# Row numbers from short lists, query units behind later lots, and a convolution whose mean products stand between its taps

## The reference

```python
def conformer_conv(h, w_pw1, b_pw1, w_dw, b_dw, ln_g, ln_b, w_pw2, b_pw2):
    a, gate = jnp.split(h @ w_pw1 + b_pw1, 2, axis=-1)
    y = a * jax.nn.sigmoid(gate)
    y = lax.conv_general_dilated(y, w_dw[:, None, :], window_strides=(1,),   # 31 taps
                                 padding=[(CONV_K // 2, CONV_K // 2)],
                                 dimension_numbers=('NWC', 'WIO', 'NWC'),
                                 feature_group_count=CONV_W) + b_dw
    y = jax.nn.silu(layernorm(y, ln_g, ln_b))
    return y @ w_pw2 + b_pw2                    # then x = x + g1 * y
...
        q = (hc @ w_query).reshape(B, T_CHUNK, PEER_HEADS, 2, PEER_DKEY // 2)
        s = jnp.einsum('bthpd,hpnd->bthpn', q, sub_keys).astype(jnp.float32)
        s_top, i_top = lax.top_k(s, PEER_TOPK)                       # 16 of 128, twice a head
        cand = (s_top[..., 0, :, None] + s_top[..., 1, None, :]).reshape(B, T_CHUNK, PEER_HEADS, PEER_TOPK * PEER_TOPK)
        cand_idx = (i_top[..., 0, :, None] * PEER_NKEYS + i_top[..., 1, None, :]).reshape(cand.shape)
        g_s, pos = lax.top_k(cand, PEER_TOPK)                        # 16 of 256
        e_idx = jnp.take_along_axis(cand_idx, pos, axis=-1)
        g = jax.nn.softmax(g_s, axis=-1)
        u = u_emb[e_idx]
        act = jax.nn.gelu(jnp.einsum('btd,bthkd->bthk', hc, u).astype(jnp.float32), approximate=False)
        return jnp.einsum('bthk,bthkd->btd', (g * act).astype(h.dtype), v_emb[e_idx])
```

## Time and profile before

| | us |
|---|---|
| median of 3 runs | 1574.71 |
| lowest and highest | 1573.56, 1574.86 |
| profiled execution | 1576.96 |
| its span in the trace | 1575.6 |
| PE, DVE, ACT, POOL busy | 1396.1, 1210.9, 733.0, 342.8 |
| mean granted clock of PE | 0.983 |

### The profile page before, as it was taken

How to read it: one execution, slowest core, us unless ns; L and a number is a source line. 1 busy time by engine, 2 the same in 40 slices (tenths; PEclk the granted TensorE clock), 3 DMA queues, 4 the chain that set the end, 5 groups by cost and what they waited for, 6 DMA issues and landing times.

```text
span 1575.6 us, 20772 instructions
## 1 busy us (share of the span) xinstructions
PE 1396.1 (89%) x7570; PEld 1022.9 (65%) x7570; DVE 1210.9 (77%) x2374; ACT 733.0 (47%) x1644; POOL 342.8 (22%) x313
## 2 busy tenths in 40 slices
PE   9899999999999999999999979978777677777776
PEld 3778899999987899998888855633332232322232
DVE  6977788887997788887785797777777777777654
ACT  4555465455577655545354544443333333333323
POOL 1100000001000000003010144555454343444430
PEclk9999999999999999999999989999999999999999
DMA  9755359998520499993432399999999999999995
GB/s 390 309 214 174 121 209 351 354 350 314 186 81 21 145 351 363 336 335 112 156 111 104 121 363 420 420 419 420 420 420 420 421 420 420 420 421 420 421 420 239
DMA packets 66199, 477.15 MB, mean 303 GB/s; under 512 B 7345, under 2 KB 7345, under 8 KB 8881
## 3 DMA queue, kind: packets, MB, share of 16 engines
q0 software_dynamic: 36864, 268.45, 41.2%
q1 hardware_dynamic: 29232, 207.37, 35.6%
q10 hardware_dynamic: 2, 0.01, 0.0%
HBM read 474.75 MB, written 1.05 MB: 302 GB/s over the span
## 4 chain that ended last, share of the span: by engine, by line
PE 49%; DMA 26%; DVE 18%; ACT 3%; issue 2%; POOL 2%; SPq 0%; DVEq 0%; POOLq 0%; ACTq 0%
DMA ring<-in_uv,crow 13%; PE ps L2054 7%; DMA row_x<-in_uv,crow 6%; PE ps L1645 6%; PE ps L1646 6%; PE ps L1647 6%; DVE HID L805 4%; PE ps L1940 4%; PE ps L1939 4%; PE ps L1937 4%; DMA row_w<-in_uv,crow 4%; DVE WB L477 3%; DMA HID<-in_uv,crow 2%; PE ps L1631 2%; DVE ring L1041 2%
## 5 line engine op out<-in xcount | busy, mean ns | idle before, releaser
L477 DVE TENSOR_TENSOR WB<-ring,WB 128x1024 fp32r<-128x1024 f32 x232 | 287.6, 1240 | 48.8 <-ACT WB L1128 45.5
L1128 ACT ACTIVATE WB<-ring 128x1024 fp32r<-128x1024 f32 x232 | 243.6, 1052 | 123.9 <-PE ps L1940 85.0
L1645 PE MATMUL ps<-hH,WB 128*128 128x256 f32 x928 | 269.7, 291 | 5.6 <-DVE WB L477 2.8
L2054 PE MATMUL ps<-ring,P 128*128 128x512 f32 x448 | 211.3, 616 | 66.9 <-ACT P L1463 66.9
L1646 PE MATMUL ps<-hL,WB 128*128 128x256 f32 x928 | 262.9, 283 | 0.0
L1647 PE MATMUL ps<-hH,WB 128*128 128x256 f32 x928 | 262.8, 283 | 0.0
L2054 PEld LDWEIGHTS ps<-ring,P 128*128 128x128 f32 x448 | 83.6, 195 | 188.8 <-ACT P L1463 102.8
L1453 ACT ACTIVATE On<-On 128x2 f32<-128x2 f32 x127 | 25.8, 203 | 375.5 <-DVE On L1041 375.5
L1041 DVE CUSTOM_DVE_ANT_0 ring<-ring,cT 128x1024 f32<-128x1024 f32 x112 | 136.3, 1225 | 77.6 <-DMA ring<-in_uv,crow 74.6
L1645 PEld LDWEIGHTS ps<-hH,WB 128*128 128x128 f32 x928 | 178.1, 192 | 10.9 <-issue 6.3
L1646 PEld LDWEIGHTS ps<-hL,WB 128*128 128x128 f32 x928 | 178.1, 192 | 2.2 <-issue 2.1
(11 more groups left out here) (304 smaller groups left out, 2747.0 us busy)
## 6 DMA issues: line engine op xcount, KB each, us to landing
ring<-in_stream SPq DMA_DIRECT2D x116, 1024.0 KB, 6.5
ring<-in_um SPq DMA_DIRECT2D x66, 1024.0 KB, 7.5
ring<-in_wm SPq DMA_DIRECT2D x4, 1024.0 KB, 12.8
bias<-in_bias SPq DMA_DIRECT2D x2, 2048.0 KB, 15.4
HID<-in_um SPq DMA_DIRECT2D x4, 512.0 KB, 17.9
ring<-in_uv,crow POOLq DMA_INDIRECT x112, 27.9
xT<-in_xT SPq DMA_DIRECT2D x1, 1024.0 KB, 8.8
cT<-in_cxT SPq DMA_DIRECT2D x1, 1024.0 KB, 14.6
```

The costliest lines, as they stand in the source:

```text
L477: ve.tensor_tensor(unit_dst(j, 1), unit_src(j), f(unit_dst(j, 0)), ALU.subtract).then_inc(s_lo, 1)
L1128: se.activation(unit_dst(j, 0), unit_src(j), ACT.Copy).then_inc(s_hi, 1)
L1645: te.matmul(o, wh[:, c], hi[:, kt, :], start=(kt == 0), stop=False)
L2054: mm = te.matmul(ps[4 + 2 * n + q][:, :], diag[:, g % 8, :], row_ap[row_of[g]][:, 1024 + q * 512:1536 + q * 512], start=(g % 128 == 0), st ...
```

## The change

In the expert layer, the first eight row numbers of route 0 come from short lists: the largest of all pair sums has to lie among the eight best of both lists, as do the seven behind it, so `first_eight` takes the eight best of either list, their 64 sums and the eight best of these. Lots 0 to 3 wait for these alone (`dve_route_first_eight`). `second_eights` then completes both lists and route 0 goes on as before; only eight of its row numbers are written by it. Before the first dot VectorE now does route 0 and the splits up to `W0+7`. Route 1 follows in steps behind dots 0 to 4, and up to lot 14 a step stands behind every dot. Queries 6 to 15 stand behind lots 3, 4, 6, 8, ... 20 (`query_lot`), five unread products ahead of mix 0, and `G1` is 50.

The last two pairs of the stream no longer go through `ring` in this stage: units 12 and 13 are loaded into `late` (which joins what were `bsp`, `wsp` and `g2row`) when the first pair of `pw2` has been split, unit 14 into a part of `bias` behind the loads for the scores, unit 15, half a pair, when the pair `L0+4` has been split. The unread products read `cols` in place of `bsp`.

In the convolution, ScalarE goes on with the next channel's diagonals and empties a channel eight diagonals later; six of the eight mean products stand between taps 14 to 19 of the last channel; one unread product follows the mean. Gate times bias is added to `xT` by VectorE ahead of the product (L865 of the change), and the product with `w_pw2` goes from PSUM into `xT` in one instruction of VectorE (L883). ScalarE converts a unit ahead of the squares, and up to the sixth tile VectorE's split stands ahead of the residual.

```diff
-        NROW, G1 = 14, 44
+        NROW, G1 = 14, 50
+        query_lot = dict(zip(range(6, 16), (3, 4, 6, 8, 10, 12, 14, 16, 18, 20)))
+        query_at = {l: k for k, l in query_lot.items()}
...
             for kt in range(8):
                 ve.tensor_tensor(yc[:, kt, :], yc[:, kt, :], ps[7][:, 0:256], ALU.subtract).then_inc(s_cen, 1)
+            for kt in range(8):
+                V.then_inc(ve.tensor_scalar(xT[:, kt, :], xT[:, kt, :], ab[:, 4, kt:kt + 1], None, ALU.add))
+            gb_in = V.n
...
-                    kt = 4 * b + u
-                    V.wait_ge(*out_a["pw2", b, u, 0])
-                    x_done.then_inc(ve.tensor_tensor(xT[:, kt, :], xT[:, kt, :], ptmp[:, kt, :], ALU.add), ("pw2", kt))
-                    unit(first["pw2", b] + u)
+                    kt, name = 4 * b + u, ("pw2", b, u, 0)
+                    if kt < 6:
+                        unit(first["pw2", b] + u)
+                    V.wait_ge(*dense[name])
...
+                    out_v.then_inc(ve.scalar_tensor_tensor(out=xT[:, kt, :], in0=row_bank(name)[:, 0:256],
+                                                           scalar=M[:, 1, 16 + kt:17 + kt], in1=xT[:, kt, :],
+                                                           op0=ALU.mult, op1=ALU.add), name)
+                    if kt >= 6:
+                        unit(first["pw2", b] + u)
...
+            def second_eights():
+                for j in range(2):
+                    V.then_inc(ve.match_replace(wk, st[:, j, 0:8], sS[0][:, j, :], GONE))
+                    V.wait_own()
+                    V.then_inc(ve.max(st[:, j, 8:16], wk))
+                    V.wait_own()
+                    V.then_inc(ve.max_index(ix[:, j, 8:16], st[:, j, 8:16], wk))
+                    V.wait_own()
+                V.then_inc(ve.tensor_copy(ixf[:, 0:2, 8:16], ix[:, 0:2, 8:16]))
+                V.wait_own()
...
             route = route_steps()
             V.wait_ge(s_const, 5)
-            for i in range(10):
+            for i in range(5):
                 next(route)
-                if i % 2 == 0:
-                    split_to(4 + i // 2)
-            split_to(9)
+                split_to(4 + i)
             for l in range(128):
                 dot(l)
-                if l % 2 == 0 and 2 <= l <= 14:
-                    split_to(l // 2 + 9)
+                if l == 3:
+                    split_to(9)
+                if l - 3 in query_at and query_at[l - 3] <= 12:
+                    split_to(query_at[l - 3] + 4)
...
-                if l % 8 < 5:
+                if l < 15 or l > 15 and l % 8 < 5:
...
-            for c, kt in enumerate(CP):
-                for k in range(31):
-                    d = 31 * c + k
-                    if d >= 8:
-                        S.wait_ge(s_tap, d - 7)
+            for d in range(len(TAPS) + 8):
+                if d >= 8:
+                    S.wait_ge(s_tap, d - 7)
+                if d < len(TAPS):
+                    kt, k = TAPS[d]
                     se.activation(dg[:, d % 8, :], ident[:], ACT.Copy, scale=wdw[:, k, kt:kt + 1]).then_inc(s_diag, 1)
-                S.wait_ge(s_tap, 31 * c + 31)
-                y_a.then_inc(se.activation(yc[:, kt, :], ps[4 + c][:, 0:256], ACT.Identity, bias=col["bdw"][:, kt:kt + 1]), kt)
+                if d in conv_emptied:
+                    kt = conv_emptied[d]
+                    y_a.then_inc(se.activation(yc[:, kt, :], ps[4 + CP.index(kt)][:, 0:256], ACT.Identity,
+                                               bias=col["bdw"][:, kt:kt + 1]), kt)
             sqrt_next()
+            ahead(first["pw2", 0])
...
-            query(6)
-            ahead(W0 + 7)
-            chosen(1)
             for l in range(128):
                 (gelu if l < 127 else gelu_last)(l)
-                if l % 2 == 0 and 2 <= l <= 18:
-                    query(l // 2 + 6)
-                    ahead(W0 + l // 2 + 7)
-                if l % 4 == 0 and 4 <= l <= 20:
-                    key_scores(l // 4 + 2)
+                if l - 1 in query_at:
+                    k = query_at[l - 1]
+                    query(k)
+                    ahead(W0 + k + 1)
+                    if k % 2:
+                        key_scores(k // 2)
...
-                G.wait_ge(s_eu, 8 * n + h + 1)
+                if l < 4:
+                    G.wait_ge(s_eu8, 1)
+                else:
+                    G.wait_ge(s_eu, 8 * n + h + 1)
...
+            for d, (kt, k) in enumerate(TAPS):
+                if k == 0:
+                    T.wait_ge(*out_v["pw1", kt // 2, 2 * (kt % 2) + 1, 0])
+                T.wait_ge(s_diag, d + 1)
+                te.matmul(ps[4 + CP.index(kt)][:, 0:256], dg[:, d % 8, :], yp[:, kt, k:k + 256],
+                          start=(k == 0), stop=(k == 30)).then_inc(s_tap, 1)
+                if kt == CP[-1] and 14 <= k < 20:
+                    mean_product(means[k - 14])
+            for kt in means[6:]:
+                mm = mean_product(kt)
             mm.then_inc(s_mean, 1)
+            T.wait_ge(s_cols, 16)
+            stand_in(ps[3], cols[:, 0:512], 1)
...
-            query(6)
+            stand_in(ps[5], cols[:, 0:512], 5)
             for l in range(128):
                 mix(l)
-                if l % 2 and l <= 17:
-                    query(7 + l // 2)
-                if l % 4 == 3 and l <= 19:
-                    key_scores(l // 4 + 3)
+                if l in query_at:
+                    query(query_at[l])
+                    if query_at[l] % 2:
+                        key_scores(query_at[l] // 2)
...
-                    elif i in (L0 + 4, L0 + 5):
-                        pair(i + 2)
+                    elif i == L0 + 4:
+                        sp.dma_start(unit_src(W0 + 15), A["stream"][L0 + 7][:, 1024:2048]).then_inc(s_late[2], 16)
...
+                        sp.dma_start(unit_src(W0 + 14), A["stream"][L0 + 7][:, 0:1024]).then_inc(s_late[1], 16)
+                    if 2 * i == first["pw2", 0]:
+                        P.wait_ge(*g_out[1])
+                        sp.dma_start(late[:], A["stream"][L0 + 6]).then_inc(s_late[0], 16)
```

More of the change, by code:

```diff
@@ L283, in mod_in, with in_ring @@
             return s_slot[4 + q % 2], 16 * (q // 2 + 2)
+        def in_ring(i):
+            return i < W0 + 12
         def unit_src(i):
+            if not in_ring(i):
+                return (late[:, 0:1024], late[:, 1024:2048], bias[:, 3072:4096], ring[:, pair_slot(L0 + 4), 0:1024])[i - W0 - 12]
             return ring[:, pair_slot(i // 2), i % 2 * 1024:i % 2 * 1024 + 1024]
@@ L289, in unit_dst, with unit_in @@
             return WB[:, i % 3, half, :]
+        s_late = [sem(f"last_query_{n}_in") for n in ("pair", "unit_14", "unit_15")]
+        def unit_in(i):
+            if in_ring(i):
+                return pair_in(i // 2)
+            return s_late[max(0, i - W0 - 13)], 16
         s_const, s_cols, s_x, s_row_c, s_c = sem("const"), sem("cols_in"), sem("x_in"), sem("crow_in"), sem("ctx_in")
@@ L313, in program @@
         m0_out = Steps(sem("dve_mod0"), ["c", "cc", "ca"])
-        x_done = Steps(sem("dve_x"), [("mlp0", k) for k in range(8)] + [("pw2", k) for k in range(8)]
+        x_done = Steps(sem("dve_x"), [("mlp0", k) for k in range(8)]
                        + [("mlp1", k) for k in range(8)] + [("fin", k) for k in range(8)])
@@ L393, in x_ready @@
             if n == "mlp1":
-                return x_done["pw2", k]
+                return out_v["pw2", k // 4, k % 4, 0]
             if n in ("fin", "b2"):
@@ L990, in route_steps @@
                     V.wait_ge(s_sc2, 2 * h + n + 1)
-                    for k in range(2):
+                    if r == 0:
+                        first_eight()
+                        yield
+                        second_eights()
+                    for k in range(2) if r else ():
                         j = 2 * h + k
```

82 lines of the change are left out of this document (48 added, 34 removed).

## The result

| | before | change |
|---|---|---|
| median of 5 runs, us | 1574.71 | 1567.67 |
| lowest and highest | 1573.56, 1577.87 | 1564.88, 1569.28 |
| profiled execution, its span | 1576.96, 1575.6 | 1569.28, 1568.0 |
| PE, DVE, ACT, POOL busy | 1396.1, 1210.9, 733.0, 342.8 | 1400.9, 1215.2, 734.4, 338.7 |

What follows compares the result with a forecast made beforehand. DMA's gathered bytes at 420.5 GB/s were taken to bound the kernel from 940 us on, TensorE before; 8.5 + 1.25 - 1.0 + 2.2 = 10.95 us gave 1566.0 profiled, 1563.8 as median, range 1560 to 1568 (1570 with Rival A).

Steps and rivals of the forecast that it cites:

- Sooner start: Start of the gather stage: row numbers from short lists come at 896.6 instead of 905.2, 8.5 us sooner (7.1 to 9.0).
- Weights out of the stage: Gather stage: fewer weight bytes move among the gathers, 0.53 MB less, 1.25 us gained (0 to 3.75).
- Dry time: Eight-row stretch: DMA waits behind TensorE's mixes and queries, 3.5 us lost (1 to 7) against 2.5 now, 1.0 worse.
- A sign that the prediction had named for being wrong: Gather stage: DMA under 400 GB/s in several stretches of 5 us between 960 and 1030 us.
- Rival A: Lots 4 to 24: the eight-row loop starves DMA throughout, 9 us lost instead of 3.5, time 1569.5; chance 0.15.
- The convolution: Convolution through the second mlp's root: reordered products, additions, conversions and splits gain 2.2 us (0.5 to 3.5).
- it passes on whole: Behind the convolution: TensorE is busy without a hole, so the whole 2.2 us gain reaches later stages.
- Rival B: Eight-row stretch: TensorE's clock falls to 1.2 GHz, 5 us lost a lot with a query, three give 1579; chance 0.04.
- C: Lots 22 to 24, now on eight rows instead of fourteen, each lose 3 us, time 1573; chance 0.06.
- rule on the shared port: Gather stage: denser route steps on VectorE would hold back GpSimd's gathers, time 1.5 us over the forecast; not adopted.

Runs made afterwards that it cites:

- whole_route: The changed kernel without its short lists, so all first gathers wait for route 0's sixteen row numbers; 0.9968 of the kernel before.
- late_pair_in_stage: The changed kernel with the weights of units 12 and 13 loaded inside the gather stage, not at the convolution; 0.9927 of the kernel before.
- change_again: The changed kernel itself, unaltered, run again beside the follow-up kernels; 0.9925 of the kernel before.
- lookup_alone: The changed kernel with the convolution's edits, from the taps to the residual of w_pw2, taken back; 0.9946 of the kernel before.
- unread_in_holes: The changed kernel with two unread products in each of two TensorE holes in the last attention; 0.9908 of the kernel before.
- conv_alone: The kernel before with only the convolution's part of the change; 0.9981 of the kernel before.

## Why the prediction was right, and where its sizes were off

**Sooner start, 8.5.** Measured 8.63 (12.91 less 4.28). Dot 0 was expected at 912.0 and came at 910.58, mix 0 at 916.2 and came at 915.32. That this is worth its full length was the sum's silent assumption. whole_route shows 0.5 to 0.6 of it in this kernel; the rest is the pair of weights that now meets the gathers and the dry time, which the sum counts in terms of their own, below.

**Weights out of the stage, 1.25.** The bytes left as stated: from the first gather to the end 271.41 MB, before 271.93. But late_pair_in_stage shows the price of 2.4 us per MB to be wrong here: nearly 0, since dry time follows.

**Dry time, "I take 3.5 us lost in all".** This is the term that was mis-sized: 6.5 in the profile, 5.3 in change_again's (50.46 less 48.21 MB), inside the bounds 1 and 7. A sign that the prediction had named for being wrong came with it, under 400 GB/s in several stretches of 5 us: 6 of the 14 from 960 to 1030 us, the lowest 283. The working had two lots with a query and scores at 10.6 us, from the 7.30 us of the earlier trace rows (its terms add up to 10.7). Measured it is 11.4 (996.10 to 1007.49), without scores 9.7. In the kernel before the scores stood behind a query of the next head. Now they stand right behind their own second query, and TensorE waits for ScalarE to empty it, in the view of waits from 940 to 1040 us:

```profile
PE ps L2135 <- ACT HID L1233: 2.6, 5, 0.5
```

A query with scores takes 4.5 us (11.39 less two mixes, 6.87), where the earlier trace rows gave 3.87: 0.65 more for each of five heads, 3.3 us, about what the term was short. That this wait is the reason is argued from the sizes; no run moved the scores alone. The order of the instructions had shown it, had I asked of each wait in a new place whether what it waits for is still being made. Rival A thus happened in part, in size between its 9 and my 3.5. Spreading the queries takes the dry time from 6.5 (47.73 MB) to 1.4 us (49.87 MB) and the time down by 3.3 to 5.4 us.

**The stage in all.** From the route's start to the end the sum had -8.75 (8.5 + 1.25 - 1.0). The profile has -6.8, the other profiles with the same stage -7.6 (late pair), -8.1, -8.3, -8.3 and, without the unread products, -8.9. With the dry time of 6.5 one expects -5.9. The 1 us between this and the profile lies ahead of the first full slice, where the sum has no term. From the first gather's issue to 940 us DMA moved 17.44 MB in 43.96 us in the change and 12.01 MB in 34.51 us before; at 420.5 GB/s that is 2.5 us lost, where it was 6.0, and of these 6.0 the prediction had counted 2.5 and left out the 3.4 up to 908.9, for which the change has 2.5. In the other profiles up to 2 us more stay open: lookup_alone and unread_in_holes, by the same sum at -6.5 and -6.2, end at -8.3. They moved 23.00 and 23.12 MB in the last 70 us, the change 22.18, so the difference lies in how the last rows land; why it varies no run shows.

**The convolution, 2.2.** Root 2.22 sooner, of 2.5 from the first tap on (0.3 was lost ahead of it); centring 1.02 sooner, where 1.45 was expected, since the product of the last-emptied channel waits 0.65 for ScalarE; the additions took 2.19 of the 2.7 allowed. "Behind it TensorE is busy without a hole, so it passes on whole" is false as it stands: there are two holes of 1.7 us, behind which the clock falls or not. In the profile of the change that took 1.4 of the 2.2 back, in conv_alone's it gave 3.2 more; by the ratios the part is worth 3.0 (1.6 to 4.3), which fits the 2.5 to 4.0 at the root.

So the 3.3 us between forecast and profile are 2.0 in the stage and 1.4 of clock. That the two ratios lie on either side of the forecast's 0.9931 is in part luck: the dry time was 1.8 to 3 us too small, and against it stood 1 us at the first gather that the sum did not have, a convolution worth up to 4.0 at the root, and an end of the stage that varies by up to 2 us. Rival B did not happen: the clock is 1.00 from 905 to 1040 us. Nor did C: from 1050 us on DMA moves 419 GB/s. The Trainium skill's rule on the shared port (SBUF — State Buffer, "SBUF: two separate sides"), by which GpSimd can't write a gather's descriptors while VectorE holds the port with a copy-like fp32 operation, shows little here when VectorE's work gets denser: of the gathers from 905 to 1100 us 26 of 80 took over 1.3 us to issue, before 23 of 83.

## What to carry to other kernels

A stage that one resource bounds at last may be bound by another at first: of the sooner first gather this kernel kept 0.5 to 0.6 until the products behind the mixes were spread out, and alone, without the first mix coming sooner, it lost. Ask of a sooner start which event frees the buffers that the stage lives on, and move that. When products are moved next to each other, ask whether the second reads what another engine still has to empty from the first. And compare a gain of 2 us over several executions: holes of 1.7 us elsewhere in this program moved single profiles by up to 4.7 us.

## What the runs showed of the hardware

The granted clock after short holes is not the same from run to run of the same instructions: after the hole of 1.73 us near 834 it was 0.50 in the change, 1.00 in change_again; behind the hole of 1.65 us near 853 it fell to 0.50 in both, and stayed 1.00 in conv_alone; behind the wait of 2.38 us at `first_eight` it was 1.00 in the change and 0.54 in change_again (897 to 899 us). A hole of 3.00 us ahead of mix 0 kept 1.00, holes of 5.67 and 8.93 us did not. So the length of a hole alone does not tell.
